# V sums of tiles 3 to 7: token-by-token gathers replaced by two passes over the whole V table with weight matrices built on the chip

## The chip, the cores and the metric

One core of a Trainium2 chip. The metric is the device time of one launch in microseconds, the median of several runs. TensorE (PE) multiplies, VectorE (DVE) and ScalarE (ACT) do the elementwise work, GpSimd (POOL) issues gathers, SyncE (SP) issues direct transfers.

## What is computed

One layer over 1152 tokens, which are 9 tiles of 128 tokens. The last part of it is a product-key expert retrieval ("PEER"), and that is what the change touches:

```python
q = (h @ peer_wq).reshape(n, PEER_HEADS, 2, PEER_HALF)
s = jnp.einsum('nhpd,hpkd->nhpk', q, peer_keys)
sc, ix = lax.top_k(s, PEER_TOPK)
...
eid = jnp.take_along_axis(cid, pos, axis=-1)      # 8 heads x 16 = 128 experts per token, of 16384
g = jax.nn.softmax(top, axis=-1)
act = jax.nn.gelu(jnp.einsum('nhkd,nd->nhk', peer_u[eid], h))
w = (g * act)
return jnp.einsum('nhk,nhkd->nd', w, peer_v[eid])
```

An expert's number is 128 x first key + second key. `peer_u` and `peer_v` are tables of 16384 rows of 1024 float32, 64 MB each. Each token needs 128 rows of U and 128 rows of V. All arithmetic is float32.

## The kernel before, in words

The work has two strands. The first is the **stages**: for each of three groups of three tiles, `norm`, `stick` (attention), `gla`, `mix`, `res` and `select`. The second strand is the **retrieval**, counted in slots, 128 slots per tile (`SLOTS`), and woven into the stages of the next group. `paces` (line 319) sets at which tick of a stage which slot is reached: slots 0 to 369 lie beside group 1's stages, slots 370 to 753 beside group 2's (384 slots), and the stages end at slot 754. A slot of the first tile weighs 0.8 of another in that plan (`LONE_U`), because no V work lies beside it: the plan puts 0.8 times as much stage work beside such a slot.

In every slot of tile j, GpSimd issues one indirect transfer (`fetch_u`, line 2539) that brings one U row for each of 128 tokens, 512 KB, to one of 8 buffers, and VectorE multiplies it with the tile's `h2` and sums (`dot`, line 2712). When a tile's 128 dots are done, ScalarE does the gelu (`gelu`), VectorE multiplies with the gates (`weigh`), and TensorE turns the weights round (`turn_weights`), all in the first slots of the next tile.

V is then done **token by token**, in slots 12 to 125 of the following tile (`value_slot`): GpSimd gathers the 128 V rows of one token (`fetch_v`, line 2549, 512 KB each), and TensorE multiplies them with a column of weights that stands alone between zeros (`set_alone`, `add_values`, line 2606: four matmuls of 512 columns with 32-column weights per pair of tokens). So while tile j's U rows are gathered, tile j-1's V rows are too: two gathers of 512 KB per slot. After slot 1152 only tile 8's V is left. V's rows go to 6 buffers, for tiles from 5 on also to the 8 buffers of the stages' weight ring, when the stages are over. VectorE ends a tile with `finish` (line 2725: gate, residual, layer norm) and GpSimd stores it.

VectorE also chooses the experts of the tiles beside the dots (`choose_beside`, line 2398): tile j+1's from slot 100 of tile j on, 12 slots a head, 8 heads; for tile 7 that is slots 868 to 963, for tile 8 slots 996 to 1091. In most slots the dots read `h2` from PSUM (`by_banks`, line 2480), in a few from SBUF. Each engine runs its instructions in the order in which they are written; a wait holds all that is behind it on its engine.

Of the kernel before, what the change touches and what calls it, by code (L numbers as in the profile page):

```python
# [97 lines left out]
ORDER = [t for g in GROUPS for t in g.tiles]  # L98

# [90 lines left out]
class Kernel:  # L190
# [5 lines left out]
    def __init__(self, nc, A, outs, ctx):  # L196
# [11 lines left out]
        self.ident = sb("ident", [P, P])  # L208
        self.from_here, self.before = sb("from_here", [P, P]), sb("before", [P, P])
# [6 lines left out]
        self.ids_of, self.ids_of_turned = sb("experts", [P, CHOSEN, SLOTS], U32), sb("expertsT", [P, CHOSEN, P], U32)  # L216
        self.gates = sb("gates", [P, CHOSEN, SLOTS])
# [1902 lines left out]
class Select:  # L2120
# [153 lines left out]
    def set_gates(self, dve, j):  # L2274
# [8 lines left out]
        gates = self.K.gates[:, j % CHOSEN, :].rearrange("p (h k) -> p h k", h=PEER_HEADS)  # L2283
        dve.tensor_tensor(gates, by_head, self.e_inv[:, :].unsqueeze(2).broadcast_to([P, PEER_HEADS, TOPK]), ALU.mult).then_inc(self.exp_done, 1)

    def choose(self, dve, j, h, s):
# [63 lines left out]
        dve.tensor_copy(self.K.ids_of[:, j % CHOSEN, cols], self.ids_f[:, cols]).then_inc(self.named, 1)  # L2350
# [66 lines left out]
class Peer:  # L2417
# [5 lines left out]
    REFILL, MORE_FROM = 16, 5  # L2423
# [5 lines left out]
    def __init__(self, K):  # L2429
# [4 lines left out]
        self.u_ring, self.v_ring = sb("u_ring", [P, NU, D]), sb("v_ring", [P, NV, D])  # L2434
        self.h2, self.x1, self.g2, self.ln2, self.prod = sb("h2", [P, 2, D]), sb("x1", [P, D]), sb("g2", [P, D]), sb("ln2", [P, 2 * D]), sb("prod", [P, D])
# [4 lines left out]
        self.u_in, self.v_in = [sem(f"u_in{r}") for r in range(NU)], [sem(f"v_in{r}") for r in range((NV + K.NW) // 2)]  # L2440
        self.h2_in, self.x1_in, self.g2_in, self.ln2_in, self.y_out = [sem(f"peer_h2_in{n}") for n in range(2)], sem("peer_x1_in"), sem("peer_g2_in"), sem("peer_ln2_in"), sem("peer_y_out")
        self.copies, self.h2_there = 0, sem("peer_h2_there")
        self.place, self.last_out = self.places(), sem("peer_last_out")
# [7 lines left out]
    def places(self):  # L2451

        more = self.K.NW
        users = [[] for _ in range(NU + NV + more)]
        for n in range(SLOTS * TILES):
            users[n % (NU + NV) if n < SLOTS else (n + self.TURN) % NU].append(("u", n))
        for m in range(P * TILES):  # L2460
            users[NU + m % NV if m < P * self.MORE_FROM else NU + m % (NV + more) if m < P * (TILES - 1) else (m + NU) % (NU + NV + more)].append(("v", m))
        return {who: (r, n + 1, had[n - 1] if n else None) for r, had in enumerate(users) for n, who in enumerate(had)}
# [17 lines left out]
    def by_banks(self, s):  # L2480

        return not any(self.K.leave_banks(G) <= s < self.K.take_banks(G) for G in GROUPS[1:])

    def free_ids(self, dve, j):
        if j >= CHOSEN:
            dve.wait_ge(self.v_used, P // 2 * (j - CHOSEN + 1))

# [17 lines left out]
    def gpsimd(self, pool):  # L2505
# [27 lines left out]
        def fetch_u(n):  # L2533
# [17 lines left out]
        for s in range(-AHEAD, SLOTS * (TILES + 1)):  # L2551
# [11 lines left out]
            if 0 <= j < TILES:  # L2563
# [4 lines left out]
            if s >= 2 * SLOTS and s % SLOTS == 48:  # L2568
                j = s // SLOTS - 2
                store(j)  # L2570
                if j + 1 < TILES:
                    load_g2(j + 1)
            if s >= 2 * SLOTS and s % SLOTS == 72 and s // SLOTS - 1 < TILES:
# [3 lines left out]
        pool.wait_ge(self.y_out, 16 * (TILES - 1))  # L2577
        for m in range(TILES * P - NU - NV - K.NW, TILES * P):
            pool.wait_ge(*self.buffer("v", m)[1:])

    def sync(self, sp):

        sp.wait_ge(self.ended, TILES)
        sp.dma_start(rows(self.K.y_out)[ORDER[-1]], self.x1[:, :]).then_inc(self.last_out, 16)
        sp.wait_ge(self.last_out, 16)
# [8 lines left out]
    def add_values(self, pe, j, i):  # L2594
# [343 lines left out]
```

## Time and profile before

| | |
|---|---|
| median of 3 runs | 4450.35 us (4444.53 to 4457.32) |
| span of the profiled execution | 4610.3 us |
| bytes moved in it | 1572 MB, 341 GB/s on average |
| PE / DVE / ACT / POOL busy | 76% / 59% / 20% / 53% |
| gathers by GpSimd (queue q0) | 1289.90 MB, 72.2% of the 16 transfer engines' span |
| direct transfers by SyncE (queue q1) | 271.38 MB, 15.8% |

The profiled execution's own time is known only as its span, from the first to the last instruction; it is 160 us above the median of the runs without a profile. "Busy" of an engine counts its executing instructions; PE's matmuls overlap, so a group's busy time is not its count times its mean. "PEclk" and the clock column are the granted TensorE clock as a share of 2.4 GHz.

### The profile page before, as it was taken

What the parts mean: (1) busy time and instruction counts of PE and PEld (TensorE: products, weight loads), DVE (VectorE), ACT (ScalarE), POOL (GpSimd) and SP (SyncE); (2) the same over time, 40 slices, a digit from 0 to 9 for tenths busy, and PEclk for the clock granted to TensorE, in tenths of its full rate; (3) what the DMA queues carried; (4) which work ended last, traced back from release to release, by engine and by line L of the source; (5) the groups of instructions that cost most, each with busy time, mean ns of one, the idle gap of its engine ahead of it and who ended that gap; (6) DMA issues with size and microseconds to landing.
All of it is one profiled execution on the core that took longest, in us unless ns stands there. A gap on an engine that the chain in (4) does not pass through costs nothing.

```text
span 4610.3 us, 46291 instructions
## 1 busy us (share of the span) xinstructions
PE 3486.6 (76%) x16122; PEld 1731.9 (38%) x16122; DVE 2734.5 (59%) x6463; ACT 911.3 (20%) x1858; POOL 2441.7 (53%) x2375
## 2 busy tenths in 40 slices
PE   7989999989899898978898988998443344433456
PEld 4656755655356443544443554434100000000011
DVE  3443412788876768775568757777843565575410
ACT  3552310134423100133444222001000000000000
POOL 0000000275777565567776766655666666666665
PEclk9999999999999899999999988998655555555567
DMA  7774452799999999999998999999999899999998
GB/s 305 285 263 191 163 164 82 277 328 329 347 377 374 384 419 400 407 351 378 391 387 321 375 358 406 407 403 393 374 378 379 336 372 377 374 370 352 375 372 316
DMA packets 422693, 1572.17 MB, mean 341 GB/s; under 512 B 47720, under 2 KB 63464, under 8 KB 411328
## 3 DMA queue, kind: packets, MB, share of 16 engines
q0 software_dynamic: 340384, 1289.90, 72.2%
q1 hardware_dynamic: 78448, 271.38, 15.8%
q10 hardware_dynamic: 3632, 7.94, 0.5%
q8 instruction: 131, 2.15, 0.2%
q14 instruction: 98, 0.80, 0.0%
HBM read 1526.42 MB, written 42.61 MB: 340 GB/s over the span
## 4 chain that ended last, share of the span: by engine, by line
PE 42%; DVE 18%; POOL 11%; another core or an unknown queue 10%; issue 9%; DMA 8%; ACT 1%; ACTq 0%; DVEq 0%; SPq 0%; POOLq 0%
PE bank L2606 7%; DVE peer_u_ring L2712 6%; PE wide L1891 6%; DMA peer_v_ring<-in_peer_v,expertsT 5%; POOL peer_u_ring L2539 4%; PE wide L1460 4%; PE wide L808 4%; POOL peer_v_ring L2549 4%; PE wide L2233 4%; PE wide L1448 3%; PE wide L871 2%; POOL w_ring L2549 2%; DMA peer_u_ring<-in_peer_u,experts 2%; PE wide L881 2%
## 5 line engine op out<-in xcount | busy, mean ns | idle before, releaser
L2539 POOL DMA_INDIRECT peer_u_ring<-in_peer_u,experts x1098 | 1153.2, 1050 | 603.0 <-issue 299.5
L2549 POOL DMA_INDIRECT peer_v_ring<-in_peer_v,expertsT x840 | 881.9, 1050 | 515.1 <-PE bank L2606 222.6
L2712 DVE SCALAR_TENSOR_TENSOR peer_u_ring<-peer_u_ring,wide 128x1024 f32<-128x1024 f32 x654 | 781.7, 1217 | 408.0 <-DMA peer_u_ring<-in_peer_u,experts 325.8
L2606 PE MATMUL bank<-peer_v_ring,peer_lone 128*32 128x512 f32 x3360 | 607.6, 730 | 450.3 <-DMA peer_v_ring<-in_peer_v,expertsT 280.9
L2606 PE MATMUL bank<-w_ring,peer_lone 128*32 128x512 f32 x1056 | 303.5, 962 | 345.7 <-DMA w_ring<-in_peer_v,expertsT 199.5
L2712 DVE SCALAR_TENSOR_TENSOR peer_u_ring<-peer_u_ring,peer_h 128x1024 f32<-128x1024 f32 x444 | 532.4, 1219 | 15.0 <-DMA peer_u_ring<-in_peer_u,experts 9.9
L2606 PEld LDWEIGHTS bank<-peer_v_ring,peer_lone 128*32 128x32 f32 x3360 | 92.8, 117 | 791.3 <-issue 771.9
L2549 POOL DMA_INDIRECT w_ring<-in_peer_v,expertsT x264 | 252.3, 956 | 141.2 <-issue 74.6
L808 PE MATMUL wide<-hT,w_ring 128*128 128x384 f32 x768 | 271.5, 501 | 6.9 <-ACT hT L589 3.6
L2606 PEld LDWEIGHTS bank<-w_ring,peer_lone 128*32 128x32 f32 x1056 | 50.5, 140 | 582.0 <-issue 576.6
L1460 PE MATMUL wide<-w_ring,hT 128*128 128x256 f32 x1152 | 260.4, 383 | 0.2 <-issue 0.2
L2508 POOL MEMSET peer_lone<- 128x1087 f32 x1 | 1.0, 1005 | 472.9 <-PEq L304 472.9
L2233 PE MATMUL wide<-mT,w_ring 128*128 128x384 f32 (+1 forms) x768 | 248.8, 476 | 0.8 <-ACT mT L2063 0.8
L1460 PEld LDWEIGHTS wide<-w_ring,hT 128*128 128x128 f32 x1152 | 216.2, 190 | 59.1 <-issue 30.8
L1225 DVE TENSOR_TENSOR sb_z<-sb_z,wide 128x768 f32<-128x768 f32 (+2 forms) x120 | 95.1, 793 | 205.5 <-PE wide L871 132.0
L1891 PE MATMUL wide<-hT,w_ring 128*128 128x384 f32 x624 | 215.6, 499 | 0.3 <-issue 0.3
L808 PEld LDWEIGHTS wide<-hT,w_ring 128*128 128x128 f32 x768 | 145.9, 196 | 110.8 <-issue 29.5
L1217 DVE SCALAR_TENSOR_TENSOR sb_l<-sb_z,sb_l 128x768 f32<-128x768 f32 (+2 forms) x120 | 95.4, 795 | 155.0 <-ACT sb_l L1092 147.2
L2233 PEld LDWEIGHTS wide<-mT,w_ring 128*128 128x128 f32 x768 | 139.9, 200 | 110.7 <-issue 36.7
L2654 ACT ACTIVATE peer_lone<-peer_wT 128x16 f32<-128x16 f32 x72 | 15.2, 225 | 815.0 <-remote 605.0
L881 PE MATMUL wide<-sb_l,before 128*128 128x384 f32 (+2 forms) x384 | 128.2, 459 | 62.8 <-DVE sb_z L1225 50.9
L871 PE MATMUL wide<-sb_l,from_here 128*128 128x384 f32 (+2 forms) x480 | 156.9, 450 | 16.3 <-DVE sb_l L1217 14.9
(332 smaller groups left out, 5204.5 us busy)
## 6 DMA issues: line engine op xcount, KB each, us to landing
w_ring<-in_weights SPq DMA_DIRECT2D x312, 512.0 KB
sb_kc<-in_kcT POOLq DMA_DIRECT2D x16, 2048.0 KB, 7.7
sb_vc<-in_vc POOLq DMA_DIRECT2D x16, 2048.0 KB, 8.6
peer_u_ring<-in_peer_u,experts POOLq DMA_INDIRECT x1098
mod_w<-in_w_ada SPq DMA_DIRECT2D x15, 1024.0 KB, 10.8
peer_v_ring<-in_peer_v,expertsT POOLq DMA_INDIRECT x840
mod_w_later<-in_w_ada SPq DMA_DIRECT2D x9, 1024.0 KB, 7.0
scores<-sel_sc SPq DMA_DIRECT2D x6, 1024.0 KB
```

The lines of the kernel that those rows point to most:

```text
L808: last = pe.matmul(out[:, 0:G.T], w[:, k, :], K.hT[:, k, 0:G.T], start=(k == 0), stop=(k == KC - 1))
L871: last = pe.matmul(r[:, h, c0:G.W], K.from_here[:, :], self.l[:, n % self.NL, h, c0:G.W], start=clears, stop=True, skip_group_check=True)
L881: last = pe.matmul(r[:, h, c0:G.W], K.before[:, :], self.l[:, n % self.NL, h, c0:G.W], start=False, stop=True, skip_group_check=True)
L1217: dve.scalar_tensor_tensor(l, self.z[:, n % self.NZ, :, c0:G.W], 0.0, l, ALU.max, ALU.add).then_inc(self.sp_ready, 1)
L1448: last = pe.matmul(out[:, 0:G.T], w[:, k, :], K.hT[:, k, 0:G.T], start=(k == 0), stop=(k == KC - 1))
L1460: last = pe.matmul(out[:, i * DV:(i + 1) * DV], K.hT[:, k, n * P:(n + 1) * P], halves[k // 4][:, k % 4, :], start=(k == 0), stop=(k == KC ...
L1891: last = pe.matmul(out[:, 0:G.T], w[:, k, :], x[:, k, 0:G.T], start=(k == 0), stop=(k == KC - 1))
L2233: last = pe.matmul(out[:, cols], w[:, k, :], K.mT[:, k, cols], start=(k == 0), stop=(k == KC - 1))
L2539: pool.indirect_dma_start(buffer, None, K.A["peer_u"], bass.IndirectOffsetOnAxis(ap=K.ids_of[:, j % CHOSEN, k:k + 1], axis=0)).then_inc(lo ...
L2549: pool.indirect_dma_start(buffer, None, K.A["peer_v"], bass.IndirectOffsetOnAxis(ap=K.ids_of_turned[:, j % CHOSEN, t:t + 1], axis=0)).then ...
L2606: last = pe.matmul(self.F.psum[strip:strip + 32, :], self.lone[:, mark - at:mark - at + 32], self.buffer("v", m)[0][:, c * HALF:(c + 1) * ...
L2712: dve.scalar_tensor_tensor(u, u, 1.0, h2, ALU.mult, ALU.mult, accum_out=self.dots[:, j % 2, k:k + 1]).then_inc(self.dot_done, 1)
```

## The change

V of tiles 0, 1, 2 and 8 stays as it was. V of tiles 3, 4, 5 (first set) and 6, 7 (second set) is computed as a dense product: each tile's weights become a matrix of 16384 experts x 128 tokens, and the whole V table is streamed past it, once per set. The matrix is built in two halves of 64 second keys. For a batch of 8 tokens of a tile:

- ScalarE makes, for each token, a 128 x 128 block of one-hot rows of the first keys (`hot_rows`: eight `Abs` of 128x128 with a bias column, then two `Relu` of 128x512: 1 - |key - i|).
- VectorE makes the 64-wide one-hot rows of the second keys times the weights (`hot_columns`: one `is_equal` and one multiply of 128x512).
- TensorE multiplies the two for each token (`build`: eight matmuls of 64 columns) into one PSUM bank, and ScalarE copies that bank into the matrix `W` (`keep_built`, 128x512).

A set of n tiles has 16n batches per half, two halves: 96 and 64 batches. After each half's batches come 64 **chunks** (`add_chunk`): SyncE loads the 128 V rows with one second key (rows j, j+128, ..., 512 KB, through 4 buffers), and TensorE adds 2 matmuls of 512 columns per tile, with 128x128 weights out of `W`, onto PSUM banks that stay open over all 128 chunks. `W` has a single buffer per set; a half's chunks must be over before the next half's batches are written. Units are laid onto slots by `planned` with the weights 3.4 per batch and 0.92 per chunk and tile: first set slots 778 to 1060, second 1062 to 1262.

```diff
-CHOSEN = 4
+CHOSEN, NAMED = 4, 2
+DENSE = ((3, 4, 5), (6, 7))
+DENSE_SLOTS = ((778, 1060), (1062, 1262))
...
     def by_banks(self, s):
-        return not any(self.K.leave_banks(G) <= s < self.K.take_banks(G) for G in GROUPS[1:])
+        return s < LAST_STAGE_SLOT and not any(self.K.leave_banks(G) <= s < self.K.take_banks(G) for G in GROUPS[1:])
...
-            if 0 <= j < TILES:
+            if 0 <= j < TILES and is_summed(j):
                 for i in range(P // 2):
                     if self.value_slot(i) == k:
                         fetch_v(j, 2 * i)
                         fetch_v(j, 2 * i + 1)
...
+    def planned(self):
+        out = {}
+        for d, tiles in enumerate(DENSE):
+            units = []
+            for half in range(self.HALVES):
+                units += [("build", d, half, b, self.BUILD) for b in range(P // self.BATCH * len(tiles))]
+                units += [("chunk", d, half, c, self.CHUNK * len(tiles)) for c in range(self.COLS)]
...
+    def stream(self, sp, lo, hi):
+        by_second = self.K.A["peer_v"].rearrange("(i j) n -> j i n", j=NKEYS)
+        for n in range(lo, hi):
+            if n == 0:
+                sp.wait_ge(self.peer.v_used, P // 2 * summed_before(DENSE_TILES[0]))
+            if n >= self.BUFFERS:
+                self.used(sp, n - self.BUFFERS)
+            sp.dma_start(self.row_buffer(n), by_second[n % P]).then_inc(self.row_in[n % self.BUFFERS].sem, 16)
...
+    def build(self, pe, d, half, b):
...
+        pe.wait_ge(*self.b_ready.at(r + 1))
+        if r:
+            pe.wait_ge(*self.w_kept.at(r))
+        for a in range(2):
+            n = self.few(d, half, b, a)
+            pe.wait_ge(*self.made(n))
+            for t in range(self.FEW):
+                at = self.COLS * (self.FEW * a + t)
+                last = pe.matmul(bank.psum[:, at:at + self.COLS], self.ones[:, n % self.A_RING, t, :], self.cols[:, r % self.B_RING, self.FEW * a + t, :], start=True, stop=True)
+            last.then_inc(self.w_full.sem, 1)
+
+    def add_chunk(self, pe, d, half, c):
...
+        pe.wait_ge(*self.row_in[n % self.BUFFERS].at(16 * (n // self.BUFFERS + 1)))
+        for i in tiles:
+            for h in range(2):
+                last = pe.matmul(self.acc(i, h).psum, self.w_of(d, i)[:, c, :], self.row_buffer(n)[:, h * HALF:(h + 1) * HALF], start=(j == 0), stop=(j == P - 1))
...
+    def scalar(self, act, s):
+        for kind, d, half, n in self.units.get(s + self.LEAD - 1, ()):
+            if kind == "build":
+                self.hot_rows(act, d, half, n)
+                if n:
+                    self.keep_built(act, d, half, n - 1)
...
+    def hot_rows(self, act, d, half, b):
...
+        for a in mine:
+            n = self.few(d, half, b, a)
+            if n >= self.A_RING:
+                act.wait_ge(*self.w_full.at(n - self.A_RING + 1))
+            for t in range(self.FEW):
+                token = at + self.FEW * a + t
+                last = act.activation(self.ones[:, n % self.A_RING, t, :], self.iota[:, :], ACT.Abs, bias=self.first_key[:, i, token:token + 1], scale=-1.0)
+            last.then_inc(self.abs_done.sem, 1)
+        for a in mine:
+            n = self.few(d, half, b, a)
+            act.wait_ge(*self.abs_done.at(self.made_by_act(n)))
+            act.activation(self.ones[:, n % self.A_RING], self.ones[:, n % self.A_RING], ACT.Relu, bias=1.0, scale=-1.0).then_inc(self.a_by_act.sem, 1)
...
+    def keep_built(self, act, d, half, b):
...
+        act.wait_ge(*self.w_full.at(self.few(d, half, b, 1) + 1))
+        built = self.K.banks[6].psum.rearrange("p (t j) -> p j t", t=self.BATCH)
+        act.activation(self.w_of(d, i)[:, :, at:at + self.BATCH], built, ACT.Copy).then_inc(self.w_kept.sem, 1)
...
+    def hot_columns(self, dve, d, half, b):
...
+        dve.tensor_tensor(out, iota.unsqueeze(1).broadcast_to(shape), self.second_key[:, i, tokens].unsqueeze(2).broadcast_to(shape), ALU.is_equal).then_inc(self.b_equal.sem, 1)
...
+        dve.wait_ge(*self.b_equal.at(r + 1))
+        dve.tensor_tensor(out, out, weights.unsqueeze(2).broadcast_to(shape), ALU.mult).then_inc(self.b_ready.sem, 1)
```

`by_act` returns True for every group of four tokens, so VectorE makes none of the first keys' rows. VectorE also splits the expert numbers into first and second keys (`set_keys`, four small instructions a tile), the sums of a dense tile are copied from PSUM by ScalarE and ended by the same `finish` at slots 1060 to 1082 and 1262 to 1276, and SyncE loads `x1` for tiles 4 to 8 and stores tiles 3 to 8. Tile 8's V goes through 12 buffers (8 of U, 4 of the weight ring) instead of 22. Expert numbers and gates are kept for 2 tiles (`NAMED`) instead of 4.

## Rows read from the trace of the kernel before

**Rows 1.** The page's part 2: the span in 40 equal slices, per engine and for the transfers.

```profile
PE   7989999989899898978898988998443344433456
DVE  3443412788876768775568757777843565575410
PEclk9999999999999899999999988998655555555567
DMA  7774452799999999999998999999999899999998
GB/s 305 285 263 191 163 164 82 277 328 329 347 377 374 384 419 400 407 351 378 391 387 321 375 358 406 407 403 393 374 378 379 336 372 377 374 370 352 375 372 316
```

**Rows 2.** Busy time of each engine by stretch, whole kernel: us busy (x instructions), clock, transfers.

```profile
864.00:1161.00 297.00, 272.18 (x1235) 169.77 (x1235) 263.19 (x639) 116.85 (x198) 162.49 (x125) 0.97 0.85 310
1161.00:1989.00 828.00, 723.57 (x3149) 384.82 (x3146) 615.61 (x1615) 155.51 (x366) 532.98 (x496) 0.94 0.99 389
2481.00:3278.00 797.00, 697.59 (x2961) 365.79 (x2959) 584.86 (x1538) 141.32 (x336) 499.14 (x479) 0.92 0.98 383
3317.00:4132.00 815.00, 321.13 (x1131) 50.96 (x1131) 466.93 (x1105) 15.13 (x35) 542.93 (x571) 0.54 0.95 369
3317.00:4610.00 1293.00, 556.18 (x2053) 95.16 (x2053) 617.22 (x1423) 26.00 (x61) 844.43 (x891) 0.57 0.93 364
```

**Rows 3.** The same stretches, VectorE's line 2712 (the dots, two instructions each) alone.

```profile
864.00:1161.00 297.00, 152.27 (x257) 0.97 0.85 310
1161.00:1989.00 828.00, 291.76 (x485) 0.94 0.99 389
2481.00:3278.00 797.00, 277.41 (x460) 0.92 0.98 383
3317.00:4610.00 1293.00, 448.44 (x748) 0.57 0.93 364
```

**Rows 4.** The stretch from 2481 us, TensorE's line 2606 (the V matmuls) alone.

```profile
2481.00:3278.00 797.00, 144.72 (x968) 21.11 (x968) 0.92 0.98 383
```

**Rows 5.** Groups of ScalarE instructions by shape: busy us, mean ns, idle before.

```profile
L1606 ACT ACTIVATE gla_kl<-gla_b 128x128 f32<-128x128 f32 x32 | 12.4, 389 | 0.0
L1589 ACT ACTIVATE gla_og<-wide 128x512 f32<-128x512 f32 x12 | 7.2, 597 | 40.8 <-PE wide L1460 40.8
L1092 ACT ACTIVATE sb_l<-sb_l 128x512 f32<-128x512 f32 x24 | 15.0, 625 | 0.3
```

**Rows 6.** Timeline of ScalarE: start us, us, instruction, a back-to-back pair, then eight key scales.

```profile
2523.38 0.80 ACT L1083 ACTIVATE sb_z<-wide 128x768 f32<-128x768 f32 x1
2524.07 0.85 ACT L1085 ACTIVATE sb_l<-sb_l 128x768 f32<-128x768 f32 x1
...
2618.16 1.97 ACT L1606 ACTIVATE gla_kl<-gla_b 128x16 f32<-128x16 f32 x8
```

**Rows 7.** Groups of VectorE instructions by shape from 2400 us: busy us, mean ns.

```profile
L2712 DVE SCALAR_TENSOR_TENSOR peer_u_ring<-peer_u_ring,wide 128x1024 f32<-128x1024 f32 x528 | 630.7, 1217 | 352.2 <-DMA peer_u_ring<-in_peer_u,experts 279.4 <-issue 69.1 <-remote 2.1
L2339 DVE TENSOR_TENSOR peer_wide<-peer_part_f,peer_sixteen 128x512 f32<-128x512 f32 x39 | 27.4, 702 | 2.9 <-DVE peer_part_f L2337 1.7
```

**Rows 8.** TensorE: 512-column matmuls as a group, then short ones in the timeline.

```profile
L2044 PE MATMUL wide<-w_ring,mT 128*128 128x512 f32 x288 | 131.6, 609 | 0.9 <-issue 0.6 <-ACT mT L2063 0.3
569.74 1.85 PE L1472 MATMUL wide<-gla_ec,gla_kl 128*128 128x16 f32 x16
573.59 3.07 PE L1472 MATMUL wide<-gla_ec,gla_kl 128*128 128x16 f32 x16 [1.84 <-DVE gla_kl L1727]
```

**Rows 9.** GpSimd's gathers from 900 to 1200 us: busy us, mean ns, idle before.

```profile
L2539 POOL DMA_INDIRECT peer_u_ring<-in_peer_u,experts x81 | 108.7, 1342 | 66.6 <-DVE peer_u_ring L2712 46.2 <-issue 20.4
```

**Rows 10.** The chain that ended last, its last pieces in order of time.

```profile
4589.50 7.27 PE bank L2606 x53
4598.02 1.24 DVE peer_prod L2730
4606.01 1.28 DVE peer_x L2748
```

More of the change, by code:

```diff
@@ L98, with is_summed, summed_before @@
 ORDER = [t for g in GROUPS for t in g.tiles]
+LAST_STAGE_SLOT = SLOTS * GROUPS[-1].first - MARGIN
+DENSE_TILES = [j for tiles in DENSE for j in tiles]
+def is_summed(j):
+    return j not in DENSE_TILES
+def summed_before(j):
+    return sum(is_summed(t) for t in range(j))
 class Arena:
@@ L2451, in places @@
     def places(self):
-        more = self.K.NW
-        users = [[] for _ in range(NU + NV + more)]
+        users = [[] for _ in range(NU + NV + K_MORE)]
         for n in range(SLOTS * TILES):
             users[n % (NU + NV) if n < SLOTS else (n + self.TURN) % NU].append(("u", n))
-        for m in range(P * TILES):
-            users[NU + m % NV if m < P * self.MORE_FROM else NU + m % (NV + more) if m < P * (TILES - 1) else (m + NU) % (NU + NV + more)].append(("v", m))
+        for m in range(P * summed_before(TILES - 1)):
+            users[NU + m % NV].append(("v", m))
+        for k in range(P):
+            at = k % (NU + K_MORE)
+            users[(at + self.TURN) % NU if at < NU else NV + at].append(("v", P * summed_before(TILES - 1) + k))
         return {who: (r, n + 1, had[n - 1] if n else None) for r, had in enumerate(users) for n, who in enumerate(had)}
@@ L2576, in gpsimd, with x1_of, prod_of, load_late @@
                 load_x1(j)
-        pool.wait_ge(self.y_out, 16 * (TILES - 1))
-        for m in range(TILES * P - NU - NV - K.NW, TILES * P):
+        pool.wait_ge(self.y_out, 16 * DENSE_TILES[0])
+        for m in range(P * summed_before(TILES) - NU - K_MORE, P * summed_before(TILES)):
             pool.wait_ge(*self.buffer("v", m)[1:])
-    def sync(self, sp):
-        sp.wait_ge(self.ended, TILES)
-        sp.dma_start(rows(self.K.y_out)[ORDER[-1]], self.x1[:, :]).then_inc(self.last_out, 16)
-        sp.wait_ge(self.last_out, 16)
+    def x1_of(self, j):
+        return self.v_ring[:, NV - 1, :] if j == TILES - 2 else self.K.w_ring[:, K_MORE + 1, :] if j == TILES - 1 else self.x1[:, :]
+    def prod_of(self, j):
+        return self.K.w_ring[:, K_MORE, :] if j == TILES - 1 else self.prod[:, :]
+    def load_late(self, sp, j):
+        sp.dma_start(self.x1_of(j), rows(self.K.x1)[ORDER[j]]).then_inc(self.x1_late.sem, 16)
+    def store_late(self, sp, j):
+        sp.wait_ge(self.ended, j + 1)
+        sp.dma_start(rows(self.K.y_out)[ORDER[j]], self.x1_of(j)).then_inc(self.late_out, 16)
+    def sync(self, sp):
+        first, rest = DENSE
+        self.dense.begin(sp)
+        self.dense.stream(sp, 0, P)
+        self.dense.stream(sp, P, P + self.dense.BUFFERS)
+        for j in first:
+            self.store_late(sp, j)
+            sp.wait_ge(self.late_out, 16 * (j - first[0] + 1))
+            self.load_late(sp, j + 1)
+        self.dense.used(sp, P - 1)
+        for j in range(rest[0] + 1, TILES):
+            self.load_late(sp, j)
+        self.dense.stream(sp, P + self.dense.BUFFERS, 2 * P)
+        for j in range(rest[0], TILES):
+            self.store_late(sp, j)
+        sp.wait_ge(self.late_out, 16 * (TILES - first[0]))
     def turn_weights(self, pe, j):
@@ L2623, in tensor @@
                     self.turn_weights(pe, j)
-                for i in range(P // 2):
+                for i in range(P // 2 if is_summed(j) else 0):
                     if self.value_slot(i) == k:
                         self.add_values(pe, j, i)
+            self.dense.tensor(pe, s)
             yield
@@ L2638, in keep_turned @@
         out = self.F.filled(act, ("wT", j))
-        if j:
-            act.wait_ge(self.lone_ready, 8 * j)
-        act.activation(self.wT[:, :], out[:, 0:P], ACT.Copy).then_inc(self.F.kept, 1)
+        if is_summed(j):
+            if j:
+                act.wait_ge(self.lone_ready, 8 * summed_before(j))
+            kept = self.wT[:, :]
+        else:
+            kept = self.dense.keep_weights(act, j)
+        act.activation(kept, out[:, 0:P], ACT.Copy).then_inc(self.F.kept, 1)
     def set_alone(self, act, j, r):
-        n = 8 * j + r
+        n = 8 * summed_before(j) + r
         act.wait_ge(self.F.kept, self.F.at["wT", j])
@@ L2731, in finish @@
         yield
-        dve.wait_ge(self.x1_in, 16 * (j + 1))
+        if j <= DENSE_TILES[0]:
+            dve.wait_ge(self.x1_in, 16 * (j + 1))
+        else:
+            dve.wait_ge(*self.x1_late.at(16 * (j - DENSE_TILES[0])))
         dve.wait_ge(self.finish_steps, 2 * j + 1)
@@ L2761, in vector @@
                 self.weigh(dve, j - 1)
[L2762 removed]
+            if j >= 2 and k in self.END_AT and is_summed(j - 2):
                 if k == self.END_AT[0]:
```

269 lines of the change are left out of this document (236 added, 33 removed).

## The prediction

> **What bounds the kernel now.** I read the slices first [rows 1]. From about 1000 us to the end the transfers are busy 0.9 or more of the time, while TensorE is high only until about 3200 us and then at 3 to 5 tenths, at a granted clock of about half. So there are two regimes: stages with retrieval beside them, and from 3278 us retrieval alone. The stretches [rows 2] put numbers to it, and the dots [rows 3] tell which slots they are: 257 instructions are 128 slots, 485 are 242, 460 are 230. The stretch 2481 to 3278 us is slots 524 to 754 (group 2's later stages): transfers 0.98 busy at 383 GB/s, TensorE 698 of 797 us, VectorE 585. From 3317 us (slot 778) to the end it is transfers at 0.93 and nothing else above half. Bytes bound both, but in the first one TensorE and VectorE stand close behind.
>
> All sums are made against the profiled span, 4610.3 us. The median without a profile is 4450.35, a factor of 0.9653, with which I carry the result over. A measurement of this kernel tells a change of some 0.3% from none (4437 to 4464 us).
>
> **Part 1, the V gathers of tiles 3 to 7 go; slots 524 to 754 lose theirs.** Over the kernel five gathered tiles (5 x 67 MB) become two streamed tables (2 x 67 MB): 201 MB less. In this stretch 230 V gathers go and nothing takes their place. What is late next? TensorE's work without the V matmuls is 697.6 - 144.7 = 553 us [rows 2, 4], VectorE's stays 585 us. The stretch at 864 us is the one with stages and U gathers alone: there TensorE was busy 272 of 297 us (0.92) and VectorE 263 (0.89). At these shares TensorE's work wants 603 us and VectorE's 660. A second way, by pace: 297 us / 128.5 slots = 2.31 us, and as a slot there carries 0.8 of the stage work, 2.89 per full slot, against 828 / 242.5 = 3.41 with V gathers beside [rows 2, 3]: a ratio of 0.85, or 675 us. I take 660, so **-137 us**; ends 603 (-194) and 740 (-57, if waits between the engines grow). GpSimd issues one gather a slot instead of two; 1.34 us each is the worst row [rows 9], under the 2.8 us of a slot.
>
> **Part 2, the batches: 96 in the first set, 64 in the second.** ScalarE first. The eight `Abs` are 128x128 with a bias column: 389 ns each by the like row [rows 5]; back-to-back instructions overlap by 0.80 - 0.69 = 0.11 us, and eight smaller ones of that kind (72 columns on average) took 1.97 us [rows 6]. So 8 x 0.28 = 2.25 us. Two `Relu` of 128x512 at 0.625 - 0.11 make 1.03, the copy of a 128x512 bank at 0.597 - 0.11 makes 0.49 [rows 5]. Sum 3.8 us. TensorE: eight short matmuls with full weights; sixteen of that sort took 1.85 us at a high clock and 3.07 at a lower one [rows 8], so 0.9 to 1.5 us, and up to twice the first, 1.85, at half clock. It hides beside ScalarE except for one link: there is one bank and a ring of three groups of four, so ScalarE's second four `Abs` wait for TensorE's first four of the batch before, which wait for the copy just made. Against the 1.13 us of four `Abs` stand four short matmuls, their way through the array and two signals, so a wait of 0 to 1 us. I take 0.3: **4.1 us a batch**. VectorE: two 128x512 operations at 0.70 [rows 7] = 1.4 us, and the dots that `planned` lays beside a batch, 3.4 x 282 / 680 = 1.41 slots x 1.24 us = 1.75: 3.15, under ScalarE. But where it also chooses experts it is the later one: its work after 3317 us other than dots is 617 - 448 = 169 us [rows 2, 3], less four tile ends of 9.3 us (4598.0 to 4607.3 us) [rows 10] 132 us over 160 slots, 0.82 us a slot; a batch then takes 3.15 + 1.16 = 4.3, I take 4.5. This meets slots 919 to 963 and 1062 to 1091. Per half: 48 x 4.1 = 197; 32 x 4.5 + 16 x 4.1 = 210; 20 x 4.6 + 12 x 4.1 and part of three tile ends = 160; 32 x 4.1 = 131. **698 us**; ends 160 x 3.8 = 608 and 160 x 4.8 = 768. Transfers are half idle in them, as 1.4 U gathers per 4.1 us is 180 GB/s, and only 4 V buffers can be filled ahead. That is the price of the change.
>
> Here the Trainium skill ("ScalarE: Activation LUTs", Rules for kernel authors) says to do `relu` and the like on VectorE. By the rows that would move the first keys' rows to VectorE at 2 x 0.70 us, 3.15 + 1.4 = 4.55 us a batch, later than ScalarE's 4.1, so in this kernel the rule would cost some 70 us; the trace does not bear it out for a VectorE that has the dots too.
>
> **Part 3, the chunks, 128 per set.** TensorE: 131.6 us / 288 = 0.457 us per 512-column matmul at a clock near full [rows 8]; six a chunk are 2.74 us, four are 1.83. Transfers: a chunk of the first set has 0.92 x 3 x 282 / 680 = 1.145 slots beside it, so 2.145 x 0.524 = 1.125 MB. Slices reach 419 GB/s where direct and gathered transfers mix, the stretch average is 389 [rows 1, 2]; at 410 this is 2.74 us, a tie. I take 2.8 us: 358 us. Second set, first half: 42 U slots + 64 V = 55.6 MB, 136 us (TensorE 117). Second half: 64 + 46 gathers of tile 8 = 57.7 MB, 141 us. Together **635 us**; ends 620 (419 GB/s, TensorE's 351 in the first set) and 750 (below).
>
> No row before shows reads at the pitch of the V stream, rows 512 KB apart. The Trainium skill ("DMA: Bandwidth & Descriptors", Latency and other measured facts) gives 207 GB/s per direction for such a pitch against 214 at full rate; by that 3% the sum would be some 10 us longer, an estimate from the page.
>
> **Part 4, set-up and tail.** `set_keys` is twelve small instructions and the first batch fills a pipeline: 8 us. After the last chunk come the last V pairs and three tile ends in a row instead of one: 13.5 us from the last matmul to the end today (4596.8 to 4610.3 us) [rows 10] + 2 x 9.3 + 8 for the pairs: **40 us**. Without cost: `h2` read from SBUF (the dots took 1.18 us a slot in the stretch at 864 us, where many read it there, and 1.20 in the last stretch [rows 3]), SyncE's direct issues (its queue is free after the stages), the stores of tiles 3 to 5, which hold up SyncE's stream only while batches are built; if they didn't fit there, some 10 us.
>
> **Sum.** From slot 778 on: 8 + 698 + 635 + 40 = 1381 us against 1293 today, +88. With part 1: 4610 - 137 + 88 = 4561 us, x 0.9653 = **4403 us**, 1.1% faster. Bytes fall by 13%, but the second regime becomes one of alternating phases, engines and then bytes.
>
> **Rivals.**
> 1. *Both bounds meet their floors.* The stage stretch goes to TensorE's 603 us (-57 more) and batches to ScalarE's bare 3.8 with VectorE's choosing absorbed (625 us, -73): 4431, x 0.9653 = 4278 us. For it: TensorE ran near 1.00 of time in stages without retrieval (slices 5 to 7) [rows 1]. Against: VectorE has 585 us in that stretch. 22%.
> 2. *Slower, by the link copy, TensorE, ScalarE.* With TensorE mostly idle between batches its clock stays near 0.54, as it did at 321 busy of 815 us [rows 2], and the wait in every batch is 1 us instead of 0.3: 4.8 us on 108 batches, +0.3 on the others, +92 us: 4653, so 4492 us. It decides from about +63 us, a batch of 4.5 to 4.6 us. For it: one bank, three groups. Against: the short matmuls at 3.07 / 16. 13%.
> 3. *Slower, the V stream starved in the chunks.* Eight U gathers stand against four V loads. If V gets a third of 410 GB/s, a V load takes 3.8 us while the 73 slots of a half pass in 140 us; then 27 chunks are left at TensorE's 2.74: 215 us a half instead of 179, +24 and +20 in the second set: +116, 4515 us. 10%.
> 4. *An even trade*: stage stretch at 690, the rest as summed: 4425 to 4464 us. 10%.
> That the gathers stay after all is excluded by the condition in `gpsimd`.
>
> **How the numbers follow.** Forecast 45%, rivals 22, 13, 10, 10%. Faster: 0.43 + 0.22 = 0.65. Same: 0.02 + 0.10 = 0.12. Slower: 0.23. It is also open how much of the 160 us that the profile adds lies in transfers; if all, today's stretches shrink more than the batches, some 25 us against me. The range, 4275 to 4515, reaches from rival 1 to rival 3.
>
> **What would show it.** Slots 524 to 754 in 640 to 680 us with TensorE or VectorE at 0.9 and transfers near 0.75. Batches: `Abs` 0.39 us each, ScalarE busy over 0.9, transfers near half. Chunks: transfers at 0.95 or more and TensorE at full clock, near 2.8 us each in the first set. Wrong would be a batch far from 4.1 us, a V load that TensorE waits for through whole chunk phases, or a stage stretch that stays at 797 us.

## The result, and the profile after

The changed kernel takes 5132.75 us (median of 4, 5128.51 to 5135.38) against 4450.89 us: a ratio of 1.153, 95% interval 1.151 to 1.154. It is slower by 682 us where 47 us faster was forecast.

The page of the kernel after (span 5126.5 us), its busy tenths and transfer rates, as in [rows 1]:

```profile
PE   7989999888989988989798984789977998899998
DVE  3434207888777777557888887673077625721101
ACT  3542201344220013444332013830086004504500
PEclk8999999999999999999898985579955997697699
DMA  7764536889999999999678877476345754674576
GB/s 300 284 246 186 174 104 226 311 320 357 394 403 403 414 404 354 385 397 359 212 271 323 315 242 243 155 298 228 115 149 188 303 176 137 242 277 156 178 255 216
```

Up to slice 19 the two kernels look alike; in slices 20 to 24, the later stages without their V gathers, the transfers already fall from 8 or 9 tenths to between 6 and 8. From slice 26 on TensorE, which stood at 3 to 5 tenths, stands at 7 to 9, and the transfers stand between 3 and 7. The bytes did fall as the change says (1572 to 1371 MB), but in this part they are no longer the bound.

The stretches of the kernel after (columns as in [rows 2]: the length, then busy time of TensorE's matmuls, of its weight loads, of VectorE, ScalarE and GpSimd, then the granted clock, the busy share of the transfers and GB/s): the stage stretch of slots 524 to 754, everything from slot 778, then build phases and chunk phases in turn, and the tail:

```profile
2459.00:3114.00 655.00, 552.50 (x1987) 355.40 (x1987) 572.58 (x1517) 134.64 (x313) 249.13 (x234) 0.90 0.77 271
3157.00:5127.00 1970.00, 1770.24 (x5621) 1045.58 (x5620) 829.29 (x1765) 645.80 (x1775) 561.71 (x496) 0.79 0.59 204
3157.00:3390.00 233.00, 175.07 (x757) 165.32 (x757) 148.91 (x244) 185.30 (x509) 85.30 (x71) 0.50 0.52 160
3390.00:3720.00 330.00, 329.50 (x781) 146.79 (x779) 113.45 (x288) 6.59 (x21) 87.86 (x73) 1.00 0.59 220
3720.00:3950.00 230.00, 171.59 (x753) 164.02 (x753) 174.94 (x369) 185.32 (x511) 77.18 (x68) 0.50 0.50 152
3950.00:4285.00 335.00, 334.34 (x785) 148.91 (x785) 134.26 (x360) 9.00 (x23) 94.46 (x77) 0.99 0.61 223
4285.00:4450.00 165.00, 115.71 (x502) 109.20 (x502) 143.40 (x311) 126.25 (x343) 60.12 (x49) 0.51 0.56 181
4450.00:4670.00 220.00, 220.00 (x518) 97.57 (x516) 47.27 (x79) 5.45 (x18) 47.95 (x45) 1.00 0.70 261
4670.00:4840.00 170.00, 158.98 (x724) 111.89 (x723) 41.52 (x60) 122.67 (x341) 48.70 (x52) 0.53 0.51 162
4840.00:5090.00 250.00, 250.00 (x728) 97.82 (x725) 0.00 (x0) 1.77 (x5) 53.45 (x57) 0.99 0.72 245
5090.00:5127.00 37.00, 15.06 (x85) 4.07 (x84) 25.54 (x60) 3.46 (x6) 6.69 (x7) 0.72 0.45 156
```

The stage stretch went from 797 us [rows 2] to 655, with transfers at 0.77. After slot 778 the batches take 233 + 230 + 165 + 170 = 798 us and the chunks 330 + 335 + 220 + 250 = 1135 us. In every chunk phase TensorE is busy to the last microsecond at full clock, and the transfers stand at 0.59 to 0.73.

TensorE's timeline in the first chunk phase shows the price of a chunk: 12 instructions, 5.15 us from one chunk to the next (3402.49 to 3407.64). The program issues 6 matmuls there.

```profile
3401.63 1.02 PE L3003 MATMUL bank<-peer_v_ring,dense_w 128*128 128x512 f32 x2
3402.49 4.45 PE L3003 MATMUL wide<-peer_v_ring,dense_w 128*128 128x512 f32 x10
3406.78 1.02 PE L3003 MATMUL bank<-peer_v_ring,dense_w 128*128 128x512 f32 x2
3407.64 4.46 PE L3003 MATMUL wide<-peer_v_ring,dense_w 128*128 128x512 f32 x10
```

The timeline of one batch, all engines (some lines left out):

```profile
3302.18 0.57 ACT L3063 ACTIVATE dense_w<-wide 128x512 f32<-128x512 f32 x1
...
3302.66 1.26 ACT L3046 ACTIVATE dense_a<-dense_iota,dense_first 128x128 f32<-128x128 f32 x4
...
3302.85 3.65 PE L2987 MATMUL wide<-dense_b,dense_a 128*128 128x64 f32 x16 [1.23 <-ACT dense_w L3063]
...
3304.83 1.28 ACT L3046 ACTIVATE dense_a<-dense_iota,dense_first 128x128 f32<-128x128 f32 x4 [0.91 <-PE wide L2987]
3306.01 1.13 ACT L3051 ACTIVATE dense_a<-dense_a 128x512 f32<-128x512 f32 x2
...
3307.05 0.57 ACT L3063 ACTIVATE dense_w<-wide 128x512 f32<-128x512 f32 x1
```

A batch is a circle of 4.87 us (3302.18 to 3307.05), and it goes through both engines. TensorE starts 0.67 us after the copy's start. ScalarE's second four `Abs` wait for TensorE's first eight instructions and start 1.98 us later (3304.83). Behind them, in ScalarE's order, come the two `Relu` (1.18 us later) and the next copy (1.04 us later). TensorE's other eight instructions are over at 3306.50, before ScalarE gets to the copy, so they aren't what holds it. TensorE waits 1.23 us for the copy, ScalarE 0.91 us for TensorE. Eight matmuls in the program are again sixteen instructions, 3.65 us at a clock of 0.50.

### The profile page after: what moved, and what is told of

Same layout as the page of the kernel before. It is cut to its first block, busy times and chain, and to the rows that moved or that the text cites. A ratio compares the mean times of both kernels' runs of the same rounds, so it can differ in the third digit from the quotient of the medians.

```text
span 5126.5 us, 52860 instructions
## 1 busy us (share of the span) xinstructions
PE 4529.9 (88%) x18682; PEld 2666.2 (52%) x18682; DVE 2938.9 (57%) x6800; ACT 1530.8 (30%) x3568; POOL 1888.7 (37%) x1725
## 4 chain that ended last, share of the span: by engine, by line
PE 65%; DVE 16%; ACT 8%; DMA 5%; issue 3%; POOL 3%; PEldq 0%; DVEq 0%; SPq 0%; ACTq 0%; PEld 0%; POOLq 0%
PE wide L3003 20%; PE wide L1907 7%; PE wide L2987 6%; DMA peer_v_ring<-in_peer_v,expertsT 4%; DVE peer_u_ring L2768 4%; PE wide L1476 4%; PE bank L2653 4%; PE wide L824 3%; ACT dense_a L3046 3%; PE wide L2249 2%; ACT dense_a L3051 2%; PE wide L1464 2%; PE bank L3003 2%; PE wide L887 2%; PE bank L1907 2%
## 5 line engine op out<-in xcount | busy, mean ns | idle before, releaser
L2768 DVE SCALAR_TENSOR_TENSOR peer_u_ring<-peer_u_ring,peer_h 128x1024 f32<-128x1024 f32 x842 | 1007.0, 1219 | 59.1 <-DMA peer_u_ring<-in_peer_u,experts 57.1
L3003 PE MATMUL wide<-peer_v_ring,dense_w 128*128 128x512 f32 x2304 | 1026.7, 597 | 2.5 <-ACT dense_w L3063 2.5
L2987 PE MATMUL wide<-dense_b,dense_a 128*128 128x64 f32 x2560 | 575.5, 418 | 184.9 <-ACT dense_w L3063 158.9
L3003 PEld LDWEIGHTS wide<-peer_v_ring,dense_w 128*128 128x128 f32 x2304 | 437.9, 191 | 568.5 <-issue 567.6
L2987 PEld LDWEIGHTS wide<-dense_b,dense_a 128*128 128x128 f32 x2560 | 550.0, 326 | 247.2 <-issue 166.6
L2571 POOL DMA_INDIRECT peer_v_ring<-in_peer_v,expertsT x384 | 426.5, 1111 | 219.4 <-PE bank L2653 118.6
L3046 ACT ACTIVATE dense_a<-dense_iota,dense_first 128x128 f32<-128x128 f32 x1280 | 406.0, 389 | 270.5 <-PE wide L2987 229.2
L3125 DVE TENSOR_TENSOR dense_b<-dense_iota,dense_second 128x512 f32<-128x512 f32 x160 | 110.5, 690 | 471.6 <-PE wide L2987 471.6
L2768 DVE SCALAR_TENSOR_TENSOR peer_u_ring<-peer_u_ring,wide 128x1024 f32<-128x1024 f32 x256 | 304.9, 1213 | 58.0 <-DMA peer_u_ring<-in_peer_u,experts 57.2
L2653 PE MATMUL bank<-peer_v_ring,peer_lone 128*32 128x512 f32 x1536 | 215.2, 636 | 101.6 <-DMA peer_v_ring<-in_peer_v,expertsT 95.7
```

Source lines behind the costliest of these rows:

```text
L2571: pool.indirect_dma_start(buffer, None, K.A["peer_v"], bass.IndirectOffsetOnAxis(ap=K.ids_of_turned[:, j % CHOSEN, t:t + 1], axis=0)).then ...
L2653: last = pe.matmul(self.F.psum[strip:strip + 32, :], self.lone[:, mark - at:mark - at + 32], self.buffer("v", m)[0][:, c * HALF:(c + 1) * ...
L2768: dve.scalar_tensor_tensor(u, u, 1.0, h2, ALU.mult, ALU.mult, accum_out=self.dots[:, j % 2, k:k + 1]).then_inc(self.dot_done, 1)
L2987: last = pe.matmul(bank.psum[:, at:at + self.COLS], self.ones[:, n % self.A_RING, t, :], self.cols[:, r % self.B_RING, self.FEW * a + t, : ...
L3003: last = pe.matmul(self.acc(i, h).psum, self.w_of(d, i)[:, c, :], self.row_buffer(n)[:, h * HALF:(h + 1) * HALF], start=(j == 0), stop=(j ...
L3046: last = act.activation(self.ones[:, n % self.A_RING, t, :], self.iota[:, :], ACT.Abs, bias=self.first_key[:, i, token:token + 1], scale=-1.0)
```

## The experiments

**A second profile of the kernel before.** 

> The kernel before, unchanged, for a second profiled execution. The first one's span was 4610 us where the runs are 4450. If the 160 us are the profile's own cost, this span is again near 4610; if they were an accident of that one execution, it is near 4450, and the slots after 1000 us, bound by transfers, are where the difference lies (778 to the end in about 1200 us instead of 1293).

No edit. Time 4453.84 us, ratio 0.9995 (0.998 to 1.001), profiled span 4448 us:

```profile
2460.00:3252.00 792.00, 697.02 (x2955) 365.28 (x2955) 585.26 (x1538) 141.39 (x336) 492.11 (x480) 0.92 0.99 386
3291.00:4448.00 1157.00, 477.61 (x2053) 59.14 (x2053) 623.54 (x1423) 25.96 (x61) 841.42 (x890) 0.53 1.00 407
```

So the 160 us belong to that one execution and are not the profile's cost, and 136 of them lie after slot 778 (1293 against 1157 us): 364 GB/s there against 407. The stage stretch is nearly the same, 797 and 792, though its transfers are as full. Why that one execution moved bytes more slowly stays open. Against this execution the change costs -137 us in the stage stretch and 1970 - 1157 = +813 after slot 778, together +676; the two spans differ by 678.

**Half of the chunk matmuls.**

```diff
-            for h in range(2):
+            for h in range(2 if j in (0, P - 1) else 1):
                 last = pe.matmul(self.acc(i, h).psum, self.w_of(d, i)[:, c, :], ...
```

> Edit: in all chunks but the first and the last of a set, only columns 0 to 511 of V are multiplied (3 and 2 matmuls a chunk instead of 6 and 4); columns 512 to 1023 of tiles 3 to 7 are left out of the sums. V is still streamed whole. Theory A (TensorE bounds the chunk phases, each 512-column float32 matmul costs it about 0.85 us as two instructions of 0.43): the first set's chunk phases fall from 340 us to about 180 to 190 each (then the transfers hold them), the second set's from 230 and 245 to about 135 to 150; the whole by 480 to 520 us, to about 4630 us. Theory B (the V stream, in rows 512 KB apart and beside the gathers, bounds them): nothing moves by more than 30 us, 5100 to 5135 us.

4652.6 us, ratio 1.045 (1.042 to 1.048), 480 us less than the kernel after. The first set's chunk phases, which took 330 and 335 us:

```profile
3390.00:3565.00 175.00, 172.24 (x407) 75.84 (x407) 120.60 (x296) 8.79 (x24) 86.44 (x75) 0.99 1.02 414
3790.00:3970.00 180.00, 176.28 (x419) 78.79 (x418) 135.64 (x354) 7.19 (x18) 88.19 (x76) 0.97 1.01 408
```

They fall by half, and now the transfers too are full, at 414 and 408 GB/s. This is theory A, and it is also what the prediction had priced: a chunk at 2.74 us of TensorE and a tie with the transfers. Without knowing it, the prediction had priced a kernel that does half the multiplication.

**Almost no V stream.**

```diff
-            sp.dma_start(self.row_buffer(n), by_second[n % P]).then_inc(...)
+            wide = D if n < self.BUFFERS else 32
+            sp.dma_start(self.row_buffer(n)[:, 0:wide], by_second[n % P][:, 0:wide]).then_inc(...)
```

> Edit: after the first four of 256 V loads, each load brings 32 of 1024 columns of its rows, so almost none of the V table is moved; matmuls and builds as they are, on stale rows. Theory A: the chunk phases stay at 340, 340, 230 and 245 us and the whole within 20 us of 5130. Theory B: the first set's chunk phases fall towards what the U gathers need, 73 slots x 1.4 us = 100 us plus nothing, so the whole falls by several hundred us.

5137.4 us, ratio 1.154 (1.151 to 1.158), the same as the kernel after. A chunk phase of each set:

```profile
3390.00:3725.00 335.00, 334.12 (x789) 149.47 (x789) 118.84 (x299) 7.32 (x19) 95.47 (x76) 0.99 0.37 127
4450.00:4680.00 230.00, 227.08 (x545) 103.19 (x545) 53.97 (x89) 11.30 (x31) 54.02 (x48) 0.98 0.33 117
```

Transfers drop to 0.37 and 0.33 and not one microsecond comes back. Theory B, a V stream that starves the chunks (rival 3), falls.

**The batches: four kernels.** First (run e3) a second PSUM bank for the last 32 batches, so that TensorE need not wait for the copy:

```diff
+    def build_bank(self, d, half, b):
+        return self.K.banks[5 if d == 1 and half == 1 and b % 2 else 6]
...
-            pe.wait_ge(*self.w_kept.at(r))
+            pe.wait_ge(*self.w_kept.at(r - (d == 1 and half == 1 and b > 0)))
```

> Edit: in the last half (32 batches) the build's matmuls alternate between two PSUM banks, so TensorE need not wait for ScalarE's copy of the batch before. Theory C (a batch is the chain copy, wait, sixteen short matmul instructions at half clock, copy; 4.85 us): the stretch of these batches falls from 155 us to 125 to 135, the whole by 20 to 30 us to about 5105. Theory D (ScalarE's own work holds the batch): the same stretch stays within 5 us, the whole at 5130.

5122.2 us in two runs, some 10 us less than after; the phase itself goes from 171 to 163 us. A part of it:

```profile
4675.00:4815.00 140.00, 136.74 (x622) 96.32 (x620) 37.38 (x54) 106.69 (x299) 41.32 (x44) 0.54 0.53 172
```

The gain is a third to a half of what theory C asked. The row says why: TensorE is busy 137 of 140 us at a clock of 0.54, for tile 8's V matmuls lie in this phase too. In the kernel after it was already busy 159 of 170 us there, so the phase had little to give, and this run says little about the three others.

Then (run e4) half of the first keys' rows on VectorE:

```diff
     def by_act(self, n):
-        return True
+        return n % 2 == 0
```

> Edit: of each batch's two groups of four one-hot rows, VectorE makes one (one 128x512 comparison, 0.69 us) and ScalarE only the other. Theory C' (TensorE's sixteen short instructions at half clock, 3.65 us, and the copy behind them set the batch): the batch stays at 4.5 to 4.9 us and the whole within 40 us of 5130. Theory D (ScalarE's own 3.8 us set it): ScalarE's part falls to 2.1 us, the batch to what VectorE needs, about 3.9 us, and the whole by 100 to 150 us.

5088.5 us, ratio 1.143 (1.140 to 1.146): 44 us less, just outside the 40 of theory C' and far from the 100 to 150 of D. Most of the first build phase, and one batch of it (copy, TensorE, the next copy; other lines left out):

```profile
3160.00:3365.00 205.00, 170.45 (x749) 162.99 (x749) 164.92 (x276) 112.40 (x280) 86.08 (x67) 0.50 0.57 170
3250.02 0.60 ACT L3063 ACTIVATE dense_w<-wide 128x512 f32<-128x512 f32 x1 [1.96 <-PE wide L2987]
...
3250.72 3.65 PE L2987 MATMUL wide<-dense_b,dense_a 128*128 128x64 f32 x16 [0.73 <-issue]
...
3254.40 0.60 ACT L3063 ACTIVATE dense_w<-wide 128x512 f32<-128x512 f32 x1 [1.96 <-PE wide L2987]
```

ScalarE is down to 112 of 205 us, TensorE's 170 are what they were. Now the circle is the one of theory C': the copy starts 0.03 us behind TensorE's sixteenth instruction, and a batch takes 4.38 us (3250.02 to 3254.40). Taking ScalarE's second four `Abs` and one `Relu` off the circle is worth 0.49 us a batch: the first phase falls from 234 to 210 us. Over all four the gain is 38 us; the third, where TensorE waits for VectorE, grows from 164 to 171.

Every build matmul twice (run e5):

```diff
-            for t in range(self.FEW):
+            for t in [t for t in range(self.FEW) for _ in range(2)]:
```

> Edit: every build matmul is issued twice in a row with the same operands and result (32 short instructions a batch instead of 16). If the chain through TensorE sets the batch and the clock stays at half: 4.85 + 3.65 = 8.5 us a batch, +580 us, about 5710. If the clock rises because TensorE is busier: 32 x 0.115 = 3.7 us a batch at full clock, the batch stays near 4.9 us and the whole within 30 us of 5130; that would say that full clock alone would take about 1.8 us off TensorE's part of a batch. If ScalarE holds the batch (theory D): somewhere between, since the doubled work would at half clock fill 7.3 us.

5582.6 us, ratio 1.254 (1.251 to 1.258), +450:

```profile
3160.00:3525.00 365.00, 330.49 (x1500) 323.02 (x1499) 147.30 (x241) 191.86 (x515) 81.73 (x69) 0.50 0.32 99
3303.70 0.60 ACT L3063 ACTIVATE dense_w<-wide 128x512 f32<-128x512 f32 x1 [1.10 <-PE wide L2987]
...
3304.39 7.06 PE L2987 MATMUL wide<-dense_b,dense_a 128*128 128x64 f32 x32 [0.73 <-issue]
...
3311.49 0.60 ACT L3063 ACTIVATE dense_w<-wide 128x512 f32<-128x512 f32 x1 [1.10 <-PE wide L2987]
```

A batch takes 7.79 us (3303.70 to 3311.49), less than the 8.5 expected: all 32 instructions lie on the circle now, where in the kernel after only the first eight did. TensorE is busy 0.91 of the time and the granted clock stays at 0.50. My second case, that more work would raise the clock, did not happen.

Last (run e8), one-hot rows and weighted columns in bfloat16 (this rounds the weights; W and V stay float32):

```diff
-        self.ones = room.sb("dense_a", [P, self.A_RING, self.FEW, P])
-        self.cols = room.sb("dense_b", [P, self.B_RING, self.BATCH, self.COLS])
+        self.ones = room.sb("dense_a", [P, self.A_RING, self.FEW, P], BF16)
+        self.cols = room.sb("dense_b", [P, self.B_RING, self.BATCH, self.COLS], BF16)
```

> Edit: one-hot rows and weighted columns of the batches in bfloat16 (the weights are rounded to 8 bits, the one-hot rows are exact), the matrix W and the V rows stay float32. TensorE's part of a batch becomes eight short instructions instead of sixteen. Theory C': the batch falls from 4.8 us to ScalarE's own 3.8 to 4.0, the four build phases from 768 us together to 620 to 650, the chunk phases stay (340, 340, 230, 245); the whole near 5000 us. Theory D: the builds stay within 20 us of 768.

4964.5 us, ratio 1.115 (1.112 to 1.118), 168 us less. Most of the first build phase, and the last chunk phase:

```profile
3150.00:3330.00 180.00, 27.04 (x371) 20.87 (x368) 141.33 (x232) 179.97 (x513) 83.94 (x68) 0.50 0.62 195
4670.00:4930.00 260.00, 260.00 (x790) 101.02 (x788) 4.56 (x9) 4.05 (x9) 58.18 (x62) 1.00 0.73 247
```

TensorE's work in the first build phase goes from 175 us to 27 (this window ends just short of the phase), its instructions from 757 to 371: one per matmul instead of two. ScalarE is now busy all of the time, 180 of 180 us, and the phase is 185 us or 48 x 3.85: the prediction's 3.8 us of ScalarE work per batch is its floor. The four build phases take 637 us together instead of 803. The chunks, still float32, did not move. So in the kernel after the batch was set by the circle through both engines, 4.87 us; behind it stands TensorE with the copy alone, 4.38, and behind that ScalarE alone, 3.85.

**The whole dense product in bfloat16 (run e6).** V rows too: ScalarE copies each float32 row buffer into a bfloat16 one. This changes the computation's precision for tiles 3 to 7.

```diff
+    def cut_row(self, act, d, half, c):
+        n = P * d + self.COLS * half + c
+        act.wait_ge(*self.row_in[n % self.BUFFERS].at(16 * (n // self.BUFFERS + 1)))
...
+        act.activation(self.row_cut[:, n % self.CUT, :], self.row_buffer(n), ACT.Copy).then_inc(self.cut_done, 1)
...
-        pe.wait_ge(*self.row_in[n % self.BUFFERS].at(16 * (n // self.BUFFERS + 1)))
+        pe.wait_ge(self.cut_done, n + 1)
```

> Edit: the whole dense product in bfloat16: one-hot rows, weighted columns, W, and the V rows, which ScalarE copies from the float32 buffers into bfloat16 ones (1.04 us per chunk). Theory A: the chunk's matmuls fall to a quarter, 6 x 0.21 = 1.3 us, and the chunk phases become bound by transfers, about 180, 180, 135 and 145 us; with builds at 3.9 us a batch (625 us) the stretch from slot 778 takes some 1310 us and the whole is 4440 to 4490 us, about the time of before. If a chunk were bound by the V stream's row pitch, its phases would stay above 250 us in the first set.

4495.7 us (4491.7 to 4498.8), ratio 1.009 (1.008 to 1.011). Its first four phases:

```profile
3165.00:3350.00 185.00, 28.15 (x384) 21.80 (x384) 146.29 (x239) 184.40 (x524) 86.90 (x69) 0.50 0.63 198
3350.00:3515.00 165.00, 99.54 (x379) 35.32 (x385) 112.36 (x275) 70.34 (x73) 79.49 (x71) 0.93 1.02 413
3515.00:3705.00 190.00, 28.43 (x379) 21.31 (x377) 178.59 (x388) 183.55 (x522) 83.76 (x70) 0.51 0.66 214
3705.00:3875.00 170.00, 96.41 (x385) 34.74 (x393) 121.75 (x315) 71.76 (x74) 83.60 (x70) 0.95 1.01 408
3400.21 1.04 PE L3006 MATMUL wide<-dense_rows,dense_w 128*128 128x512 bf16 x4 [1.03 <-ACT dense_rows L3042]
...
3401.30 0.38 PE L3006 MATMUL wide<-dense_rows,dense_w 128*128 128x512 bf16 x1
```

Of a chunk's six matmuls the sixth starts 1.09 us after the first (3400.21 to 3401.30): 0.22 us each instead of 5.15 / 6 = 0.86, a quarter. The phases now alternate as the prediction had pictured: ScalarE, then transfers at 1.02 and 413 GB/s. From 3165 us to the end it takes 1332 us, where the prediction had 1381. And still this is 1% slower than the kernel before, whose last stretch is 1157 us: in the build phases, half of the time, the transfers stand at 0.63 and 0.66 (in the two shown) behind ScalarE.

**The phases laid over each other (run e9).** W in bfloat16 takes half the room, so it can stand twice: the batches of each half are built beside the chunks of the half before.

```diff
+STRETCHES = ((('build', 0, 0, 778, 868),), (('chunk', 0, 0, 868, 968), ('build', 0, 1, 869, 967)), (('chunk', 0, 1, 968, 1090), ('build', 1, 0, 990, 1089)), (('chunk', 1, 0, 1116, 1194), ('build', 1, 1, 1117, 1193)), (('chunk', 1, 1, 1194, 1262),))
...
-        self.W = Arena(K.nc, (SBUF_TO - 4 * tall * self.COLS * P) // 32 * 32, SBUF_TO).sb("dense_w", [P, tall, self.COLS, P])
+        self.W = Arena(K.nc, (SBUF_TO - 4 * tall * self.COLS * P) // 32 * 32, SBUF_TO).sb("dense_w", [P, 2 * tall, self.COLS, P], BF16)
...
+    def w_of(self, d, half, i):
+        return self.W[:, {(0, 0): (3, 4, 5), (0, 1): (0, 1, 2), (1, 0): (3, 4), (1, 1): (5, 2)}[d, half][i]]
```

> Edit: the bfloat16 dense product of e6, and W in two copies (it takes half the room), so that the batches of each half are built beside the chunks of the half before instead of after them; the slots are laid out anew. Theory A with the serial phases as the remaining loss: ScalarE's sum of work after slot 778 is 160 x 3.8 + 256 x 0.95 = 850 us and the transfers' 397 MB at 410 GB/s 970 us; laid over each other the five stretches take about 190 + 250 + 290 + 190 + 190 and the tail 40, 1150 us instead of e6's 1334: the whole about 4310 us, 3% under the kernel before. If the phases were not what costs (theory: a shared limit such as the memory ports slows both when they overlap), it stays near 4495 us.

4321.5 us (4320.6 to 4323.8), ratio **0.971** (0.969 to 0.972): 3% faster than the kernel before and 16% faster than the one after. From slot 778 on:

```profile
3157.00:4322.00 1165.00, 557.66 (x3022) 203.12 (x3069) 824.03 (x1770) 885.22 (x2042) 599.82 (x498) 0.73 0.92 345
```

1165 us instead of 1332, with the transfers at 0.92. The stretch is now as long as the one of before (1157), and the stage stretch's gain is what is left over.

The 3% are not won with the same arithmetic: five of nine tiles sum V in bfloat16 here, all of them in float32 in the kernel before. In float32 laying the phases over each other could not have been enough. TensorE is busy 1770 of the 1970 us after slot 778 in the kernel after; 621 of these lie in the build phases at a clock of 0.50 to 0.53, and had they run at full clock, some 1460 us would be left, an estimate from these rows, against the 1157 us of before.

The same with every fourth group of rows made by VectorE (`return n % 4 != 3`). 

> Edit: e9, and VectorE makes every fourth group of four one-hot rows instead of ScalarE. ScalarE's work falls by 80 x 1.7 = 136 us minus the share that VectorE had to give: where ScalarE ends last (first and fourth stretch) a gain of 20 to 40 us, where VectorE does (second and third, with the choosing of experts) a loss of as much; the whole within 30 us of e9.

4319.5 us, ratio 0.970 (0.968 to 0.972), no difference from e9. ScalarE is busy 770 instead of 885 us and nothing comes back. That the transfers, at 0.92, are what is left is likely, but no run tried it.

## Why the prediction was wrong, step by step

**The step that failed: part 3, "0.457 us per 512-column matmul".** [rows 8] gives 131.6 us for 288 *instructions*. A float32 matmul of the program is two of them, as the chunk's timeline (12 for 6) and the bfloat16 builds (371 for 757) show. A chunk of the first set costs TensorE 5.15 us, not 2.74, and one of the second 220 / 64 = 3.4, not 1.83. The chunks took 1135 us instead of 635: 500 of the missed 589 us after slot 778, and halving the chunk matmuls gave 480 us back. The means to see it were in my own rows: [rows 4] counts 968 instructions of line 2606 in 230 slots, where the program issues 4 per pair of tokens, about 460. I even wrote that TensorE and transfers tie; the factor of two turned the tie into a bound. Half the chunk matmuls gave 175 us for a phase put at 179, so the transfer side of part 3 stands. The all-bfloat16 kernel's 1332 us for a stretch put at 1381 are nearer than the parts deserve: its batches go at ScalarE's pace without the wait that part 2 had, which alone is some 46 us.

**Part 2, the batch, was 4.1 us and is 4.87.** The same factor: a batch is sixteen short instructions, not eight, so 3.65 us at half clock and not 1.5 to 1.85. The term that failed is the wait of ScalarE for TensorE, put at 0.3 us: it is 0.91. The link itself (copy, TensorE's first four matmuls, ScalarE's second four `Abs`) is as the prediction drew it. The durations of ScalarE (0.389, 0.613, 0.574 us in the kernel after against 0.389, 0.625, 0.597 of [rows 5]) and its sum of 3.8 us held. So the mechanism was rival 2's, with its wait of 1 us and its 4.8 us a batch; the batches with their set-up took 798 us against 698 + 8, and rival 2 had asked 92 more. In part that was luck: it counted eight instructions too, and it gave as reason for the low clock a TensorE mostly idle between batches, where TensorE was busy 175 of 233 us at 0.50.

**The scale was wrong too.** I set a sum of engine times against a span that was 3.6% longer than the runs and multiplied all by 0.9653. The second profile shows that 136 of the 160 us lay in the last stretch alone. Against its 792 and 1157 us my own 660 and 1381 are -132 and +224, and 4448 - 132 + 224 = 4540 us: slower by 2%, before any error in a matmul. I had named this as "some 25 us against me"; it was 4540 - 4403 = 137 us, and it had the sign of the result.

**What held.** The stage stretch: 660 us forecast, 655 measured, with VectorE at 573 of 655 and transfers at 0.77. The tail: 40 us forecast, 37 in the last row, and 30 from the end of the last chunk's matmuls (5096.8). That GpSimd and SyncE's loads cost nothing: the thin stream changed no phase, and GpSimd was busy 562 of 1970 us. Rival 3 fell (thin stream). Rival 1 fell too: the stage stretch took 655 us and not 603, and a batch reached ScalarE's bare pace only once its operands were bfloat16. So did rival 4, with its 690 us for the stage stretch.

By the Trainium skill ("DMA: Bandwidth & Descriptors", Latency and other measured facts) a row pitch of 512 KB costs 3%, measured there on rows of 16 KB. The trace does not contradict it: the chunk phases with half the matmuls ran at 414 GB/s, of 419 at best in [rows 1], and since about half of their bytes are U gathers, 3% of the rest would not stand out. By the Trainium skill ("ScalarE: Activation LUTs", Rules for kernel authors) `relu` and the like belong on VectorE. Half of the first keys' rows there gained 44 us in this kernel, though 70 us of loss was my figure for all of them; in the overlapped kernel a quarter there changed nothing.

## What to carry to other kernels

Before a group's busy time is divided by its count, hold the count against the program: so many instructions of that line in so many steps. Where the two differ, the price is per instruction and the program's operation costs several. Trading bytes for matmuls paid here only once the matmuls were short and lay beside the remaining transfers: phases that alternate between an engine and the transfers cost their sum, and laying them over each other was worth 174 us, where bfloat16 alone stopped 1% short of break-even. In a ring of waits between two engines, follow the start times once round before naming the engine that sets it: here half of TensorE's instructions did not count, and taking four `Abs` away from ScalarE helped although ScalarE was waiting. A row that TensorE is busy nearly all of a phase, as in the last build phase, says beforehand that cutting a wait there will tell little. And where a profiled span is away from the median of the runs, don't scale the whole sum: take a second profile, or treat the difference as lying in one regime and compute both cases.

## What the runs showed of the hardware beyond that

TensorE's granted clock stays at 0.50 (1.2 GHz) through whole build phases, even with TensorE busy 330 of 365 us in matmuls of 64 columns whose weight loads take as long (323 us), and it is at 0.99 to 1.00 in the chunk phases of 512 columns right behind them. So a high busy share in these rows did not go with the full clock; why it stayed down in the build phases was not tried. A float32 matmul with 128x128 weights was two instructions in every trace here: 0.43 us each at 512 columns and full clock, 0.86 us together, against one of 0.22 us in bfloat16. A bfloat16 result from float32 inputs made VectorE's 128x512 comparison no faster: 0.689 us in the bfloat16 kernel, 0.690 in float32.
